# Down projections: one 512-column matmul into two banks' halves, or two 256-column matmuls into one sum

## The chip, the cores and the metric
The kernel runs on one core of one Trainium2 chip. The metric is the device time of one execution in microseconds (us); lower is better. It is one program: a decoder trunk of two layers, batch 1, 256 tokens, width 2048, all data in float32.

## The reference, cut to what matters
Nine products of the trunk end in an update of the residual stream x, each with a gate vector per feature:

```
x = x + g1 * ((u * sv) @ w_out)            # gMLP mixer, layer 0: 4096 -> 2048 features
x = x + g1 * (attention @ w_o)             # layer 1: 2048 -> 2048
x = x + g2 * ((silu(a) * v) @ w_down)      # both layers: 5632 -> 2048
```

The kernel calls all of them down projections (kind `dn`). The two gMLP halves (2048 rows each), the attention output, and for each layer three slices of the feed-forward (2048, 2048 and 1536 rows) make nine phases: `sgu_o0`, `sgu_o1`, `wo`, `dn00` to `dn02`, `dn10` to `dn12`. The rest of the trunk (up projections, key/value and query projections, spatial mixing, attention, the norms and the modulation vectors) isn't touched by the change.

## The kernel before, in words
**Precision.** Each float32 operand is split into a high half, which is what the type float32r holds, and a low half, the rest. A product is high weights times high activations, high weights times low activations, and low weights times high activations. Activations lie as `[128, tile, 512]`: columns 0 to 255 are the high half of the 256 tokens, 256 to 511 the low half (`h_op` for inputs of up projections, `act_op` for those of down projections).

**Weights.** All weights come as one stream of 1 MB pieces into four slots (`raw`). SyncE issues the loads and waits on the semaphore `stream`, which VectorE raises when it has done with half a piece. ScalarE rounds each half piece into `w_hi` (L923), VectorE subtracts it to get `w_lo` (L1091), four slots each. Between them come pieces of the modulation matrices, which VectorE multiplies and sums by itself (L1107). The order of weight halves (`s`), modulation pieces (`m`) and work on the previous chunk's result (`E`, `U`) is written out by hand for each chunk as a string of tokens, such as `sssEsEsEsmmssEm`; every engine walks the same strings.

**Tiling.** A chunk is 512 output features, four tiles of 128 (`TPC`). A down phase has four chunks, of eight half pieces each (six in `dn02` and `dn12`), 36 chunks and 272 half pieces in all. A half piece carries two tiles (k = 0, 1) of the inner dimension. For each of the four output tiles j, TensorE does two matmuls of 512 columns with the high weights (L1518) and then two of 256 columns with the low weights (L1522). Each has its own weight load. So in the bank of an output tile, columns 0 to 255 gather hi x hi and lo x hi, columns 256 to 511 gather hi x lo. That makes 2176 matmuls of each line on `act_op`. Chunks alternate between banks 0 to 3 and 4 to 7, so the result of one is read while the next is computed.

**Updating x.** VectorE's `update_x` (L1195) adds a chunk's result to x. For each output tile it does two instructions (L1211), one for each half of the bank: x = gate * half + x. It is 8 instructions a chunk, 288 in all. Normally, at the token `E` with number 0 of the next chunk it does the four for the first halves (`UPDATES[0]`), at number 1 the four for the second (`UPDATES[1]`), which raise `xlow`. The bank group is free again for TensorE when `xlow` has been raised four times for the chunk (`free_rule`, L236). At the token `U`, and where the next phase begins with a norm of x (`up00`, `kv`, `up10`), all eight are done together (`"all"`). After the last chunk both groups run, one behind the other, and the output transfers wait for `xlow`.

**Start of a phase with a norm.** ScalarE squares the last four tiles of x as `xlow` releases them (L965), TensorE sums the squares over partitions (L1433, L1436), ScalarE takes the root (L968), VectorE inverts it (L1155) after two weight halves, then both write the new `h_op` (L1175, L974, L1181). The first matmuls of the phase (L1506, L1509) wait for that.

Of the kernel before, what the change touches and what calls it, by code (L numbers as in the profile page):

```python
# [26 lines left out]
P = 128  # L27
D = 2048
T = 256
# [15 lines left out]
TPC = COLS // P  # L45
# [8 lines left out]
ALU, ACT, AX = mybir.AluOpType, mybir.ActivationFunctionType, mybir.AxisListType  # L54
# [229 lines left out]
def build(nc, io, stop=None):  # L284
# [7 lines left out]
    with ctx:  # L292
# [11 lines left out]
        x = sb("x_res", [P, KT, T])  # L304
# [20 lines left out]
        banks = ctx.enter_context(nc.psum_tensor("banks", [P, 8, 512], F32))  # L325
# [19 lines left out]
        def sem(name):  # L345
            return ctx.enter_context(nc.semaphore(name))
# [42 lines left out]
        prod = sem("prod")  # L389
        ahi = sem("ahi")  # L390
        alo = sem("alo")
        xup = sem("xup")
        xlow = sem("xlow")
        vread = sem("vread")
        v_copied = sem("v_copied")
# [51 lines left out]
        def vec(slice_, kt):  # L447

            return modv[:, slice_, kt:kt + 1] if isinstance(kt, int) else modv[:, slice_, bass.ds(kt, 1)]
# [51 lines left out]
        def done_wait(eng, prev):  # L501
# [2 lines left out]

        UPDATES = {0: [(0, j) for j in range(TPC)], 1: [(1, j) for j in range(TPC)],
                   "all": [(0, 0), (0, 1), (1, 0), (0, 2), (1, 1), (0, 3), (1, 2), (1, 3)]}

        def h_tiles(e):  # L510

# [563 lines left out]
        def _(dve):  # L1075
# [119 lines left out]
            def update_x(which, prev):  # L1195

                g = group(prev)
                gate, n = GATE_OF[PHASE_OF[id(prev.first)]], prev.first.n["xup"]
                if which != 1:
                    dve.wait_ge(mod_ready, ready_after(gate))  # L1200
                    if n:
                        dve.wait_ge(xlow, TPC * n)
                for part, j in UPDATES[which]:
                    if part:
                        dve.wait_ge(xup, TPC * n + j + 1)
                    elif j < TPC - 1:
                        dve.wait_ge(tile_done, (TPC - 1) * n + j + 1)
                    else:
                        done_wait(dve, prev)
                    kt = TPC * prev.first.loc + j  # L1210
                    dve.scalar_tensor_tensor(  # L1211
                        out=x[:, kt, :], in0=banks[:, g + j, T * part:T * (part + 1)], scalar=vec(gate, kt),
                        in1=x[:, kt, :], op0=ALU.mult, op1=ALU.add).then_inc(xlow if part else xup, 1)

            def evacuate(e, name, cur, prev, first):

# [171 lines left out]
        def _(pe):  # L1388
# [32 lines left out]
            def step(name, cur, prev, first):  # L1421
# [20 lines left out]
                for tok, t in enumerate(cur.first.tokens):  # L1442
# [8 lines left out]
                    if kind in ("v", "kvt", "vh"):  # L1451

                        pair, g = (u, g) if kind != "vh" else (2 * cur.first.loc + u % 2, 2 * (u // 2))
                        fresh_k, last_k = 0, KT - 1
                        if kind == "vh":
                            run = [r for r in range(5) if RUN_STARTS[r] <= cur.first.hs][-1]
                            fresh_k = 4 * BY_NAME["head"][RUN_STARTS[run]].loc
                            last_k = 4 * BY_NAME["head"][RUN_ENDS[run]].loc + 3
                            if u < 2:
                                pe.wait_ge(h_ready, 2 * (pair + 1))  # L1460
                            if run and cur.first.hs == RUN_STARTS[run] and u % 2 == 0:
                                if run <= 2:
                                    pe.wait_ge(v_copied, 4 * (run - 1) + u // 2 + 1)
                                else:
                                    pe.wait_ge(v_added, 4 * (run - 3) + u // 2 + 1)
                        hi = w_hi[:, slot, :].rearrange("p (k c) -> p k c", k=2)
                        lo = w_lo[:, slot, :].rearrange("p (k c) -> p k c", k=2)
                        for n in range(2):
                            for k in range(2):
                                kt = 2 * pair + k  # L1470
                                a_hi, a_lo = (operand[:, kt, o + P * n:o + P * (n + 1)] for o in (0, T))
                                out = banks[:, g + n, :]
                                pe.matmul(out, a_hi, hi[:, k, :], start=(kt == fresh_k), stop=False,  # L1473
                                          skip_group_check=True)
                                pe.matmul(out, a_hi, lo[:, k, :], start=False, stop=False, skip_group_check=True)  # L1475
                                last = pe.matmul(out, a_lo, hi[:, k, :], start=False, stop=(kt == last_k),  # L1476
                                                 skip_group_check=True)
                    elif kind == "gate":
                        hi = w_hi[:, slot, 0:KT * NGATE].rearrange("p (k c) -> p k c", k=KT)
                        lo = w_lo[:, slot, 0:KT * NGATE].rearrange("p (k c) -> p k c", k=KT)  # L1480
                        for kt in range(KT):
                            pe.matmul(banks[0:NGATE, g, :], hi[:, kt, :], operand[:, kt, :], start=(kt == 0),
                                      stop=False, skip_group_check=True)
                            last = pe.matmul(banks[0:NGATE, g, 0:T], lo[:, kt, :], operand[:, kt, 0:T],
                                             start=False, stop=(kt == KT - 1), skip_group_check=True)
                    elif kind == "cmp":
                        hi = w_hi[:, slot, :].rearrange("p (l c) -> p l c", l=8)
                        lo = w_lo[:, slot, :].rearrange("p (l c) -> p l c", l=8)
                        i = u // 4
                        for k in range(8):  # L1490
                            row = 8 * (u % 4) + k
                            rows = blk_view(i)[:, row, :]
                            pe.matmul(banks[:, g + i, 0:2 * NB], hi[:, k, :], rows, start=(row == 0), stop=False,
                                      skip_group_check=True)
                            last = pe.matmul(banks[:, g + i, 0:NB], lo[:, k, :], rows[:, 0:NB], start=False,
                                             stop=(row == CMP_LEN - 1), skip_group_check=True)
                    else:
                        hi = w_hi[:, slot, :].rearrange("p (k c) -> p k c", k=2)
                        lo = w_lo[:, slot, :].rearrange("p (k c) -> p k c", k=2)
                        last_kt = 2 * cur.first.nsub - 1  # L1500
                        if first and u == 0 and name in H_OF:
                            for k in range(2):
                                if k:
                                    pe.wait_ge(h_ready, KT * h_index(name) + 2)
                                for j in range(TPC):
                                    pe.matmul(banks[:, g + j, :], hi[:, k, P * j:P * (j + 1)], operand[:, k, :],  # L1506
                                              start=(k == 0), stop=False, skip_group_check=True)
                                for j in range(TPC):
                                    last = pe.matmul(banks[:, g + j, 0:T], lo[:, k, P * j:P * (j + 1)],  # L1509
                                                     operand[:, k, 0:T], start=False, stop=False,  # L1510
                                                     skip_group_check=True)
                            last.then_inc(sub_done, 1)
                            u += 1
                            continue
                        for j in range(TPC):
                            for k in range(2):
                                kt = 2 * u + k
                                pe.matmul(banks[:, g + j, :], hi[:, k, P * j:P * (j + 1)], operand[:, kt, :],  # L1518
                                          start=(kt == 0), stop=False, skip_group_check=True)
                            for k in range(2):  # L1520
                                kt = 2 * u + k
                                last = pe.matmul(banks[:, g + j, 0:T], lo[:, k, P * j:P * (j + 1)],  # L1522
                                                 operand[:, kt, 0:T], start=False, stop=(kt == last_kt),
                                                 skip_group_check=True)
                            if kind == "dn" and u == cur.first.nsub - 1 and j < TPC - 1:
                                last.then_inc(tile_done, 1)
# [139 lines left out]
```

## Time and profile before

| what | value |
|---|---|
| median of 3 runs | 2592.27 us (2591.88, 2592.27, 2598.79) |
| span of the profiled execution, its own time in the profile | 2590.9 us |
| TensorE matmuls busy | 2513.3 us, 97% |
| TensorE weight loads busy | 2167.4 us, 84% |
| VectorE busy | 2152.9 us, 83% |
| ScalarE busy | 1252.1 us, 48% |
| GpSimd busy | 376.4 us, 15% |
| DMA | 685.49 MB, mean 265 GB/s |

No separate time is listed for the profiled execution beside its span. Busy time of a group of overlapping matmuls is counted once, so busy time divided by the count is not the mean duration of one.

### The profile page before, as it was taken

Reading aid. Unit: us, or ns where it says so; the run is one execution under the profiler, and the core shown is the slowest. Engines: PE = TensorE matmul, PEld = TensorE weight load, DVE = VectorE, ACT = ScalarE, POOL = GpSimd, SP = SyncE. Lnnn points to the kernel's source line nnn. Section 1 sums busy time; section 2 is a strip of 40 time slices with the busy share of each in tenths; the row PEclk is TensorE's granted clock in tenths of the full one; section 3 lists DMA queues with packets and bytes.
Section 4 is the critical chain, followed back from the end, with each engine's and each line's share of the span. In section 5 each row is a group of like instructions: output and inputs, shape, how many; then the busy total and the mean of one; then the engine's idle time right before and its main releaser. Section 6 shows DMA issues by size and latency. Waiting matters only on the chain.

```text
span 2590.9 us, 38545 instructions
## 1 busy us (share of the span) xinstructions
PE 2513.3 (97%) x14006; PEld 2167.4 (84%) x14006; DVE 2152.9 (83%) x2593; ACT 1252.1 (48%) x1654; POOL 376.4 (15%) x205
## 2 busy tenths in 40 slices
PE   6999999998999999999999999899999999999999
PEld 4878888887888888888878788688788888888887
DVE  7899898999999899988998877678989756765666
ACT  4436444535554355435544454573555435543553
POOL 0000110231120012001142200373112001200110
PEclk8999999999999999999999979899999999999999
DMA  9998788986878877887766868207677655555554
GB/s 372 368 377 321 269 329 328 338 326 245 307 283 318 324 285 283 307 330 277 283 247 249 324 250 329 103 1 293 264 287 274 238 186 195 180 193 192 182 178 147
DMA packets 94312, 685.49 MB, mean 265 GB/s; under 512 B 10465, under 2 KB 10465, under 8 KB 11233
## 3 DMA queue, kind: packets, MB, share of 16 engines
q1 hardware_dynamic: 93746, 681.27, 70.1%
q10 hardware_dynamic: 432, 2.38, 0.2%
q8 instruction: 91, 1.49, 0.2%
q14 instruction: 43, 0.35, 0.0%
HBM read 681.51 MB, written 2.10 MB: 264 GB/s over the span
## 4 chain that ended last, share of the span: by engine, by line
PE 78%; DVE 10%; DMA 6%; issue 2%; ACT 2%; POOL 0%; SPq 0%; DVEq 0%; ACTq 0%
PE banks L1518 48%; PE banks L1522 24%; DMA raw<-in_stream 6%; DVE raw L1107 3%; DVE w_lo L1091 3%; ACT w_hi L923 1%; PE banks L779 1%; PE banks L743 1%; PE banks L765 1%; DVE scratch L853 1%; PE banks L782 1%; DVE temp L1175 0%; PE banks L1473 0%; PE banks L1475 0%; PE banks L1476 0%
## 5 line engine op out<-in xcount | busy, mean ns | idle before, releaser
L923 ACT ACTIVATE w_hi<-raw 128x1024 fp32r<-128x1024 f32 x841 | 875.8, 1056 | 990.6 <-PE banks L1522 594.9
L1091 DVE TENSOR_TENSOR w_lo<-raw,w_hi 128x1024 fp32r<-128x1024 f32 x841 | 1089.9, 1318 | 309.9 <-ACT w_hi L923 307.8
L1518 PE MATMUL banks<-h_op,w_hi 128*128 128x512 f32 x3816 | 1203.0, 397 | 6.2 <-DVE w_lo L1091 5.5
L1522 PEld LDWEIGHTS banks<-h_op,w_lo 128*128 128x128 f32 x3816 | 719.0, 188 | 170.0
L1522 PE MATMUL banks<-h_op,w_lo 128*128 128x256 f32 x3816 | 752.1, 278 | 0.0
L1518 PE MATMUL banks<-act_op,w_hi 128*128 128x512 f32 x2176 | 685.8, 397 | 0.6 <-DVE act_op L1252 0.3
L1518 PEld LDWEIGHTS banks<-h_op,w_hi 128*128 128x128 f32 x3816 | 582.4, 189 | 8.4 <-issue 5.8
L1107 DVE CUSTOM_DVE_ANT_0 raw<-raw,c_all 128x2048 f32<-128x2048 f32 x224 | 554.0, 2489 | 15.7 <-ACT c_all L897 9.5
L1522 PEld LDWEIGHTS banks<-act_op,w_lo 128*128 128x128 f32 x2176 | 409.8, 188 | 96.8
L1522 PE MATMUL banks<-act_op,w_lo 128*128 128x256 f32 x2176 | 428.7, 278 | 0.0
L1518 PEld LDWEIGHTS banks<-act_op,w_hi 128*128 128x128 f32 x2176 | 332.1, 189 | 1.8 <-issue 0.9
L1343 POOL TENSOR_TENSOR temp<-temp 128x1024 f32<-128x1024 f32 x16 | 94.2, 5886 | 1156.0 <-DVE temp L1239 1156.0
L1473 PE MATMUL banks<-w_hi,h_op 128*128 128x512 f32 x320 | 127.7, 399 | 25.7 <-DVE w_lo L1091 25.7
L1475 PE MATMUL banks<-w_lo,h_op 128*128 128x512 f32 x320 | 126.4, 395 | 0.0
L1476 PE MATMUL banks<-w_hi,h_op 128*128 128x512 f32 x320 | 126.1, 394 | 0.0
L1211 DVE SCALAR_TENSOR_TENSOR x_res<-banks,mod_sums,x_res 128x256 f32<-128x256 f32 x288 | 118.3, 473 | 9.0 <-PE banks L1522 8.9
L1002 ACT ACTIVATE temp<-zpad,small 128x256 f32<-128x256 f32 x176 | 91.6, 591 | 36.8 <-DVE zpad L1229 36.8
L684 POOL TENSOR_SCALAR attn_area<-attn_area 128x15 f32<-128x15 f32 (+2 forms) x96 | 65.9, 702 | 224.1 <-DVE attn_area L674 222.6
L1473 PEld LDWEIGHTS banks<-w_hi,h_op 128*128 128x128 f32 x320 | 61.1, 191 | 41.5 <-DVE w_lo L1091 25.4
L1229 DVE TENSOR_TENSOR zpad<-banks,zpad 128x1024 f32<-128x1024 f32 x44 | 53.8, 1222 | 43.0 <-ACT zpad L996 43.0
L1234 DVE SCALAR_TENSOR_TENSOR temp<-zpad,small,temp 128x256 f32<-128x256 f32 x176 | 80.8, 482 | 3.3 <-ACT temp L1002 2.0
L1352 POOL TENSOR_TENSOR act_op<-temp,act_op 128x1024 f32 (+1 forms) x24 | 67.2, 2801 | 86.4 <-ACT act_op L1013 86.4
(162 smaller groups left out, 1379.7 us busy)
## 6 DMA issues: line engine op xcount, KB each, us to landing
raw<-in_stream SPq DMA_DIRECT2D x645, 1024.0 KB, 5.4
x_res<-in_x SPq DMA_DIRECT2D x1, 2048.0 KB, 11.3
out_x<-x_res SPq DMA_DIRECT2D x4, 512.0 KB, 5.0
mix_area<-in_w_s ACTq DMA_DIRECT2D x1, 1024.0 KB, 9.2
mix_area<-in_b_s ACTq DMA_DIRECT2D x1, 1024.0 KB, 13.8
small<-in_small SPq DMA_DIRECT2D x1, 682.0 KB, 16.3
attn_area<-in_pos ACTq DMA_DIRECT2D x1, 273.0 KB, 5.3
c_all<-in_c SPq DMA_DIRECT2D x1, 8.0 KB
```

The lines of the kernel that those rows point to most:

```text
L923: act.activation(w_hi[:, out, 0:n], raw[:, slot, half:half + n], ACT.Copy).then_inc(hi_ready, 1)
L1002: act.activation(y4[:, j, :], zpad[:, j, 2:T + 2], ACT.Identity, bias=conv_col(prev, None, j), scale=conv_col(prev, 2, j)).then_inc(tap2, 1)
L1091: dve.tensor_tensor(w_lo[:, out, 0:n], raw[:, slot, half:half + n], w_hi[:, out, 0:n].bitcast(F32), ALU.subtract).then_inc(stream, 2 if ch ...
L1107: dve.tensor_tensor_reduce(raw[:, slot, :], raw[:, slot, :], c_all[:, :], 1.0, 0.0, ALU.mult, ALU.add, out).then_inc(stream, 2)
L1211: dve.scalar_tensor_tensor(out=x[:, kt, :], in0=banks[:, g + j, T * part:T * (part + 1)], scalar=vec(gate, kt), in1=x[:, kt, :], op0=ALU.m ...
L1234: dve.scalar_tensor_tensor(out=y4[:, j, :], in0=zpad[:, j, 1:1 + T], scalar=conv_col(prev, 1, j), in1=y4[:, j, :], op0=ALU.mult, op1=ALU.a ...
L1343: pool.tensor_tensor(y, y, gt, ALU.mult).then_inc(prod, 1)
L1473: pe.matmul(out, a_hi, hi[:, k, :], start=(kt == fresh_k), stop=False, skip_group_check=True)
L1475: pe.matmul(out, a_hi, lo[:, k, :], start=False, stop=False, skip_group_check=True)
L1476: last = pe.matmul(out, a_lo, hi[:, k, :], start=False, stop=(kt == last_k), skip_group_check=True)
L1518: pe.matmul(banks[:, g + j, :], hi[:, k, P * j:P * (j + 1)], operand[:, kt, :], start=(kt == 0), stop=False, skip_group_check=True)
L1522: last = pe.matmul(banks[:, g + j, 0:T], lo[:, k, P * j:P * (j + 1)], operand[:, kt, 0:T], start=False, stop=(kt == last_kt), skip_group_c ...
```

## The change
The high weights of a down projection meet the high and the low half of the activations in two matmuls of 256 columns, each with its own weight load, and both add into columns 0 to 255 of the bank. The second half of the bank is no longer used. `update_x` then does one instruction for each tile, four a chunk, all at token `E` number 0 (or at `U`, or at the end), and these raise `xlow`; the semaphore `xup` is gone.

```diff
-        UPDATES = {0: [(0, j) for j in range(TPC)], 1: [(1, j) for j in range(TPC)],
-                   "all": [(0, 0), (0, 1), (1, 0), (0, 2), (1, 1), (0, 3), (1, 2), (1, 3)]}
+        UPDATES = {0: range(TPC), 1: (), "all": range(TPC)}
...
-                for part, j in UPDATES[which]:
-                    if part:
-                        dve.wait_ge(xup, TPC * n + j + 1)
-                    elif j < TPC - 1:
+                for j in UPDATES[which]:
+                    if j < TPC - 1:
                         dve.wait_ge(tile_done, (TPC - 1) * n + j + 1)
                     else:
                         done_wait(dve, prev)
                     kt = TPC * prev.first.loc + j
                     dve.scalar_tensor_tensor(
-                        out=x[:, kt, :], in0=banks[:, g + j, T * part:T * (part + 1)], scalar=vec(gate, kt),
-                        in1=x[:, kt, :], op0=ALU.mult, op1=ALU.add).then_inc(xlow if part else xup, 1)
+                        out=x[:, kt, :], in0=banks[:, g + j, 0:T], scalar=vec(gate, kt),
+                        in1=x[:, kt, :], op0=ALU.mult, op1=ALU.add).then_inc(xlow, 1)
...
                                 kt = 2 * u + k
+                                if kind == "dn":
+                                    for part in range(2):
+                                        pe.matmul(banks[:, g + j, 0:T], hi[:, k, P * j:P * (j + 1)],
+                                                  operand[:, kt, T * part:T * (part + 1)],
+                                                  start=(kt == 0 and part == 0), stop=False, skip_group_check=True)
+                                    continue
                                 pe.matmul(banks[:, g + j, :], hi[:, k, P * j:P * (j + 1)], operand[:, kt, :],
                                           start=(kt == 0), stop=False, skip_group_check=True)
```

## Rows read from the trace of the kernel before

**Rows 1.** The page: busy time by engine; the TensorE clock granted in 40 slices.
```profile
PE 2513.3 (97%) x14006; PEld 2167.4 (84%) x14006; DVE 2152.9 (83%) x2593; ACT 1252.1 (48%) x1654; POOL 376.4 (15%) x205
PEclk8999999999999999999999979899999999999999
```
**Rows 2.** The page: the chain that ended last, by line.
```profile
PE banks L1518 48%; PE banks L1522 24%; DMA raw<-in_stream 6%; DVE raw L1107 3%; DVE w_lo L1091 3%; ACT w_hi L923 1%; PE banks L779 1%; PE banks L743 1%; PE banks L765 1%; DVE scratch L853 1%; PE banks L782 1%; DVE temp L1175 0%; PE banks L1473 0%; PE banks L1475 0%; PE banks L1476 0%
```
**Rows 3.** Groups of the span: count, busy us, mean ns, idle before.
```profile
L1518 PE MATMUL banks<-act_op,w_hi 128*128 128x512 f32 x2176 | 685.8, 397 | 0.6 <-DVE act_op L1252 0.3 <-DVE w_lo L1091 0.2
L1522 PE MATMUL banks<-act_op,w_lo 128*128 128x256 f32 x2176 | 428.7, 278 | 0.0
L1522 PEld LDWEIGHTS banks<-act_op,w_lo 128*128 128x128 f32 x2176 | 409.8, 188 | 96.8
L1506 PE MATMUL banks<-h_op,w_hi 128*128 128x512 f32 x24 | 11.7, 638 | 14.4 <-DVE h_op L1181 14.4
L1211 DVE SCALAR_TENSOR_TENSOR x_res<-banks,mod_sums,x_res 128x256 f32<-128x256 f32 x288 | 118.3, 473 | 9.0 <-PE banks L1522 8.9
```
**Rows 4.** Groups of TensorE within `dn10`, 2028 to 2116 us.
```profile
L1518 PE MATMUL banks<-act_op,w_hi 128*128 128x512 f32 x254 | 79.8, 395 | 0.0
L1522 PE MATMUL banks<-act_op,w_lo 128*128 128x256 f32 x252 | 49.6, 278 | 0.0
```
**Rows 5.** Timeline of matmuls and loads in `dn10`: start us, length us, x merged.
```profile
2050.16 0.63 PE L1518 MATMUL banks<-act_op,w_hi 128*128 128x512 f32 x2
2050.62 0.40 PE L1522 MATMUL banks<-act_op,w_lo 128*128 128x256 f32 x2
2050.86 0.63 PE L1518 MATMUL banks<-act_op,w_hi 128*128 128x512 f32 x2
...
2050.74 0.31 PEld L1518 LDWEIGHTS banks<-act_op,w_hi 128*128 128x128 f32 x2
```
**Rows 6.** Windows `sgu_o0`, `dn10`: length, PE, PEld, DVE, ACT, POOL busy, PEclk, DMA.
```profile
332.00:421.00 89.00, 89.00 (x513) 77.72 (x512) 78.89 (x84) 36.58 (x35) 5.01 (x2) 1.00 0.87 335
...
2028.00:2116.00 88.00, 88.00 (x507) 76.76 (x506) 54.08 (x67) 37.78 (x38) 0.00 (x0) 1.00 0.55 200
```
**Rows 7.** Groups of TensorE, 248 to 265 us: the spatial mixing.
```profile
L1539 PE MATMUL banks<-mix_area,scratch 128*128 128x128 f32 x128 | 14.7, 276 | 1.9 <-DVE scratch L853 1.9
```
**Rows 8.** Timeline from `sgu_o1` to `up00`.
```profile
598.74 3.21 DVE L1211 SCALAR_TENSOR_TENSOR x_res<-banks,mod_sums,x_res 128x256 f32<-128x256 f32 x8
...
599.86 0.40 PE L1522 MATMUL banks<-act_op,w_lo 128*128 128x256 f32 x2
...
601.60 0.81 ACT L965 ACTIVATE temp<-x_res 128x256 f32<-128x256 f32 x2 [0.37 <-DVE x_res L1211]
...
604.44 1.75 DVE L1155 RECIPROCAL rstd<-rstd 128x256 f32<-128x256 f32 x1
...
607.97 2.04 PE L1506 MATMUL banks<-h_op,w_hi 128*128 128x512 f32 x4 [4.77 <-DVE h_op L1181]
```
**Rows 9.** Timeline from `dn02` to `kv`, and from `wo` to `up10`.
```profile
1349.84 3.23 DVE L1211 SCALAR_TENSOR_TENSOR x_res<-banks,mod_sums,x_res 128x256 f32<-128x256 f32 x8 [1.73 <-PE banks L1522]
...
1351.03 0.39 PE L1522 MATMUL banks<-act_op,w_lo 128*128 128x256 f32 x2
...
1837.99 3.22 DVE L1211 SCALAR_TENSOR_TENSOR x_res<-banks,mod_sums,x_res 128x256 f32<-128x256 f32 x8
...
1839.17 0.40 PE L1522 MATMUL banks<-act_op,w_lo 128*128 128x256 f32 x2
```
**Rows 10.** Timeline of the end of the kernel.
```profile
2585.38 0.39 PE L1522 MATMUL banks<-act_op,w_lo 128*128 128x256 f32 x2
...
2585.80 2.05 DVE L1211 SCALAR_TENSOR_TENSOR x_res<-banks,mod_sums,x_res 128x256 f32<-128x256 f32 x5 [0.21 <-PE banks L1522]
...
2587.88 0.33 SPq L889 DMA_DIRECT2D out_x<-x_res  x1
```

More of the change, by code:

```diff
@@ L391, in build @@
         alo = sem("alo")
-        xup = sem("xup")
         xlow = sem("xlow")
```

## The prediction
> **What bounds the kernel now.** I read the engine shares first: TensorE's matmuls are busy for 97% of the span, VectorE for 83% [rows 1]. The chain of waits agrees: 72% of it are the two matmul lines 1518 and 1522, and most of the rest is the weight stream of the first stages [rows 2]. Then the windows of single down phases, since that is where the change sits. In the densest of them for VectorE, `sgu_o0`, TensorE is busy for 89.00 of 89.00 us at a granted clock of 1.00, and VectorE for 78.89; in `dn10` it is 88.00 of 88.00 against 54.08 [rows 6]. The 2176 high matmuls on `act_op` have 0.6 us of idle time before them in the whole kernel [rows 3]. So in a down phase time is set by how often TensorE can start a matmul, and VectorE's updates lie beside it. Only at three changes of phase and at the end does TensorE stand still behind the updates [rows 8 to 10].
>
> **The matmuls.** What counts is the distance from one start to the next, not the recorded duration (397 and 278 ns), since they overlap. Two ways lead to it. Two merged matmuls are busy for one distance plus one duration. In `dn10`, line 1522 has 49.6 us for 252: 196.8 ns each, 393.7 a pair, less 278 is 115.7 ns. Line 1518 has 79.8 us for 254: 314.2 each, 628.3 a pair, less 395 is 233.3 ns [rows 4]. The timeline gives the same: two high ones take from 2050.16 to 2050.62, two low ones to 2050.86, so 0.70 us for a tile's four [rows 5]. The groups of all 2176 give 233.3 and 116.0 by the same working [rows 3].
>
> The change puts 2176 x 2 = 4352 matmuls of 256 columns where 2176 of 512 were, 2176 more with as many more weight loads. At 115.7 ns a piece the two take 231.4 ns where one took 233.3 to 233.5: 2.1 ns less, 2176 times, is 4.6 us less. It hangs on a small difference of two measured distances, so I bound it. Upper end: the starts are given in steps of 10 ns, so the pair of low ones from 2050.62 to 2050.86 may be 0.236 us or more [rows 5], 118 ns each; 2 x 118 less 233 is +3 ns, +6.5 us. Lower end: the 128-column matmuls of the spatial mixing take 14.7 us for 128, 114.8 ns each with the gap in them [rows 7]; if 113 is what a full 128-column load allows, it is -7.3 ns, -16 us.
>
> The new weight loads: does a load keep up with 116 ns, six times in a row, where it did so twice and then had 233 ns twice? A load is recorded with 188 ns [rows 3], more than 116, but the two loads recorded from 2050.74 together take 0.31 us, so the second began 0.12 us after the first, and they overlap [rows 5]. The spatial mixing had 128 loads and 128 matmuls of 128 columns in a row at 114.8 ns [rows 7]. So the pace is known to hold, also for the supply of instructions, which goes from 8 to 12 in 0.70 us, 58 ns each; the mixing used one every 57 ns. I cost the loads at nothing beyond the distance.
>
> TensorE's page of the Trainium skill speaks against the split. "TensorE: Matmul & The Clock Gate", section "Back-to-back issue gap", gives the gap at the full clock as columns over 2.4 GHz and 2.5 ns on top, for each matmul. By it, an estimate, two halves would cost 2.5 ns more than one whole, +5.4 us over 2176, and the sum below would come out 10 us higher. The trace has 115.7 and 233.3 instead, above the rule's 109 and 216, and shows no fixed part: twice the short distance is less than the long one [rows 4].
>
> **The updates.** 288 instructions take 118.3 us of VectorE, 0.41 us each in a row [rows 3]; half of them go, 59 us. In the middle of a phase that is worth nothing, because TensorE has no idle time there [rows 6]; its cover is TensorE's own row, and cover grows rather than shrinks. Nothing waits longer either: `xlow` comes four instructions earlier, so banks and GpSimd's squares are released sooner, and no wait is added. The stream gets its slots sooner; it only fills slots that TensorE doesn't need yet.
>
> At the three changes of phase the updates stand on the path: squares, sum, root, inverse and the new `h_op` all hang on the last `xlow` [rows 8]. From `sgu_o1` to `up00` eight updates run from 598.74 to 601.95. The last tile's sum is complete at about 600.26, the end of the pair at 599.86; the other three updates are done by about 599.97. The new last one starts at about 600.35 and ends at 600.82, 1.13 us earlier. From `dn02` to `kv`: sum complete at 1351.42, last update over at about 1352.0, against 1353.07: 1.05 us. From `wo` to `up10`: complete at 1839.57, over at 1840.1, against 1841.21: 1.1 us [rows 9]. All that comes after is a chain that moves as a whole, with the weight halves ahead of the inverse (604.44) moving too. Together 3.3 us. What is late next is the same chain with its root and inverse; TensorE's stop of 4.8 us before line 1506 [rows 8] stays as long, it only begins earlier. If the weight stream, not VectorE, were what holds `up00` afterwards, about 1 us of it would be lost again.
>
> At the end, five updates run from 2585.80 to 2587.85 and the last transfer is issued at 2587.88 [rows 10]. One is left, from 2585.80 to 2586.27: 1.6 us less.
>
> **Sum.** -4.6 - 3.3 - 1.6 = -9.5 us. Against the span of 2590.9 that is 2581.4. The median of the runs shown lies 1.4 above that span, so I forecast 2582.8, 0.37% less. A difference of 0.3%, 7.8 us, is about what a measurement of this kernel can tell from no change. The forecast lies close to it.
>
> **Rivals.**
> A, the halves cost what the whole did, or each a little more: distance 116.7 to 119. Then the matmuls give 0 to +10 us, and 4.9 us is still saved: 2587 to 2597, in the middle 2590, no difference. For it: the group of all low matmuls gives 116.0, not 115.7 [rows 3], and 233.5 is twice 116.7. The skill's fixed part per matmul (same page and section) would land here too, at an estimated 2592.8. Against it: every pair read is at or under 116. 32%.
> B, slower: the pace of the loads. The pairs of fast loads are followed by slow ones now, and a row of six may run out of what was loaded ahead. Its place is every high matmul of a down phase, its price the part of a load that shows: with the busy time per 256-column matmul (196.8) in place of the distance, 2 x 196.8 - 314.2 = 79 ns more, 2176 times, +172 us less the 4.9 us that is saved, 2759 at the far end. It cancels the 4.9 us from a distance of 117.8 ns on, and passes 0.3% from 119.6 ns; a middle case of 122 is +23 us less 4.9, 2610. For it: 188 ns recorded per load against 116. Against: rows 5 and 7. 9%.
> C, a larger gain: the halves run at the 113 to 114 ns that the short matmuls of rows 7 come close to, or TensorE comes back earlier to its full clock after the three stops. The 24 matmuls of line 1506 take 638 ns against 397 [rows 3], 5.8 us in all. At -12 us for the halves it is 2575. 14%.
> The forecast itself, 2579 to 2586: 45%.
>
> **How the numbers follow.** Time 2582.8. The range runs from C's middle to A's upper end, 2574 to 2597, and leaves out B and the far end of C. For faster by over 0.3% (under 2584.5) I count all of C, three quarters of the forecast and a little of A, which bends towards the lower distances: 0.52. Within 0.3%: 0.37. Slower by over 0.3%: 0.11, B and the last of A.
>
> **What would show it.** In the profile after: 4352 matmuls of 256 columns in place of 2176, with a busy time per piece in a down phase that is one distance, 115 to 116 ns, in a row of six. A window of 88 us in `dn10` then holds some 761 matmuls, not 507. Line 1211 has 144 instructions; the runs of eight at 598, 1349 and 1838 are four, and the last `xlow` comes about 0.5 us after the last matmul; the same holds for the end. VectorE's busy time is 59 us less, with no shorter down phase to show for it. The prediction is wrong if the distance in a down phase is over 117.8 ns (no gain), if loads appear with idle matmul time between them (B), or if a stop of TensorE before line 1506 becomes longer than 4.8 us, which would eat the 3.3 us.

## The result, and the profile after

The changed kernel takes 2613.1 us (median of 4 runs, 2610.45 to 2618.37), the kernel before 2593.51 us beside it. The ratio is 1.0073, 95% interval 1.0056 to 1.009. A second comparison (`a0_changed_again`, below) gave 1.0079, 1.0064 to 1.0094. So the change costs 0.7% to 0.8%, some 20 us, where 9.5 us less was forecast. The time lies above the range (2574 to 2597).

The page of the changed kernel: busy time by engine, and the granted clock.
```profile
span 2608.7 us, 42753 instructions
...
PE 2532.5 (97%) x16182; PEld 2286.8 (88%) x16182; DVE 2086.6 (80%) x2449; ACT 1253.9 (48%) x1654; POOL 356.4 (14%) x205
...
PEclk8999999999999999999999979899999999999999
```
Against [rows 1]: 2176 more loads and matmuls, 66 us less of VectorE, the same clock row. The span is 17.8 us longer and TensorE is busy 19.2 us longer. So the lost time is in TensorE's work, and the groups say in which.

The groups of the span, as in [rows 3].
```profile
L1516 PE MATMUL banks<-act_op,w_hi 128*128 128x256 f32 x4352 | 699.8, 283 | 0.0
L1524 PE MATMUL banks<-act_op,w_lo 128*128 128x256 f32 x2176 | 438.4, 283 | 0.0
L1207 DVE SCALAR_TENSOR_TENSOR x_res<-banks,mod_sums,x_res 128x256 f32<-128x256 f32 x144 | 60.7, 477 | 16.9 <-PE banks L1524 16.3
L1502 PE MATMUL banks<-h_op,w_hi 128*128 128x512 f32 x24 | 10.1, 561 | 13.2 <-DVE h_op L1179 13.2
```
The two groups of matmuls on `act_op` were busy for 685.8 + 428.7 = 1114.5 us before; now they are busy for 699.8 + 438.4 = 1138.2 us, 23.7 us more. There is no idle time before them.

The window of `dn10` that answers to [rows 6]. Columns are length, PE, PEld, DVE, ACT, POOL busy (count), PEclk, DMA share and GB/s.
```profile
2040.00:2128.00 88.00, 88.00 (x736) 88.00 (x735) 48.69 (x54) 36.40 (x37) 0.00 (x0) 1.00 0.56 196
```
Its timeline, as in [rows 5]: start, length, instruction, x merged.
```profile
2050.24 0.64 PE L1516 MATMUL banks<-act_op,w_hi 128*128 128x256 f32 x4
2050.72 0.40 PE L1524 MATMUL banks<-act_op,w_lo 128*128 128x256 f32 x2
2050.96 0.64 PE L1516 MATMUL banks<-act_op,w_hi 128*128 128x256 f32 x4
```
A window counts every matmul that lies in it even in part, so the distance between starts is window plus one duration over the count: 88.28 us / 736 = 119.9 ns. (One matmul more or less in the count moves a distance by 0.2 ns here and by 0.5 ns in the windows of 512 columns below, and a tile of a window of 88 us by 1 to 1.4 ns.) The timeline agrees: four from 2050.24, two from 2050.72, the next at 2050.96, six in 0.72 us. A tile takes 720 ns. Before it was (88.00 + 0.3) / 507 x 4 = 696.6 ns [rows 6]. 761 matmuls in 88 us had been forecast. The loads are now busy for all of the window.

The change from `sgu_o1` to `up00`, as in [rows 8].
```profile
605.14 0.40 PE L1524 MATMUL banks<-act_op,w_lo 128*128 128x256 f32 x2
...
612.08 1.58 PE L1502 MATMUL banks<-h_op,w_hi 128*128 128x512 f32 x4 [4.38 <-DVE h_op L1179]
```
From the start of the last pair of down matmuls to the first of the next phase it is 6.94 us, against 607.97 - 599.86 = 8.11 us: 1.17 us less, where 1.13 was forecast. Of this, 0.39 us is a shorter stop before the first matmul, 4.38 us against 4.77; the forecast had the stop as long as before. The same distance at the other two changes shrank by 1.11 us each, counted from the start of the last down matmul (6.90 and 6.82 us against 8.01 and 7.93), where 1.05 and 1.1 were forecast.

The end of the kernel, as in [rows 10].
```profile
2604.77 0.40 PE L1524 MATMUL banks<-act_op,w_lo 128*128 128x256 f32 x2
...
2605.72 0.33 SPq L887 DMA_DIRECT2D out_x<-x_res  x1
```
From the last pair to the last transfer it is 0.95 us against 2.50: 1.55 us less, 1.6 forecast.

### The profile page after: what moved, and what is told of

It reads as the page before. It is cut to its first block, busy times and chain, and to the rows that moved or that the text cites. A ratio compares the mean times of both kernels' runs of the same rounds, so it can differ in the third digit from the quotient of the medians.

```text
span 2608.7 us, 42753 instructions
## 1 busy us (share of the span) xinstructions
PE 2532.5 (97%) x16182; PEld 2286.8 (88%) x16182; DVE 2086.6 (80%) x2449; ACT 1253.9 (48%) x1654; POOL 356.4 (14%) x205
## 4 chain that ended last, share of the span: by engine, by line
PE 83%; DVE 8%; DMA 5%; issue 2%; ACT 2%; POOL 0%; SPq 0%; DVEq 0%; ACTq 0%
PE banks L1520 32%; PE banks L1524 26%; PE banks L1516 20%; DMA raw<-in_stream 5%; DVE raw L1105 2%; DVE w_lo L1089 2%; DVE temp L1173 1%; ACT w_hi L921 1%; PE banks L777 1%; PE banks L741 1%; PE banks L1469 1%; PE banks L1471 1%; PE banks L1472 1%; PE banks L763 1%; DVE scratch L851 1%
## 5 line engine op out<-in xcount | busy, mean ns | idle before, releaser
L1516 PE MATMUL banks<-act_op,w_hi 128*128 128x256 f32 x4352 | 699.8, 283 | 0.0
L1516 PEld LDWEIGHTS banks<-act_op,w_hi 128*128 128x128 f32 x4352 | 600.4, 192 | 0.5 <-issue 0.4
L1105 DVE CUSTOM_DVE_ANT_0 raw<-raw,c_all 128x2048 f32<-128x2048 f32 x224 | 545.7, 2452 | 14.2 <-ACT c_all L895 9.6
L1524 PE MATMUL banks<-act_op,w_lo 128*128 128x256 f32 x2176 | 438.4, 283 | 0.0
L1524 PEld LDWEIGHTS banks<-act_op,w_lo 128*128 128x128 f32 x2176 | 339.4, 192 | 0.0
L682 POOL TENSOR_SCALAR attn_area<-attn_area 128x15 f32<-128x15 f32 (+2 forms) x96 | 65.9, 703 | 228.3 <-DVE attn_area L672 226.7
L994 ACT ACTIVATE zpad<-banks 128x1024 f32<-128x1024 f32 x44 | 45.1, 1026 | 68.5 <-PE banks L1524 68.5
```

Source lines behind the costliest of these rows:

```text
L1105: dve.tensor_tensor_reduce(raw[:, slot, :], raw[:, slot, :], c_all[:, :], 1.0, 0.0, ALU.mult, ALU.add, out).then_inc(stream, 2)
L1516: pe.matmul(banks[:, g + j, 0:T], hi[:, k, P * j:P * (j + 1)], operand[:, kt, T * part:T * (part + 1)], start=(kt == 0 and part == 0), sto ...
```

## The experiments

### The two halves of the change, each alone

**Split, but two sums** (`e1_split_two_halves`), on the kernel before:
```diff
+                                if kind == "dn":
+                                    for part in range(2):
+                                        pe.matmul(banks[:, g + j, T * part:T * (part + 1)],
+                                                  hi[:, k, P * j:P * (j + 1)],
+                                                  operand[:, kt, T * part:T * (part + 1)],
...
```


> The kernel before with the high matmul cut into two of 256 columns, each still adding into its own half of the bank, and x updated in eight instructions as before. It is the split without the single sum. The profile of the changed kernel shows 120.0 ns from start to start in all six matmuls of a tile (720 ns) where the kernel before has 696.6. Theory F, a fixed part of about 13.3 ns for every load and matmul beyond its columns at 2.4 GHz (256 columns 106.7, 120.0 measured; 512 columns 213.3, 226.5 measured in the key and value projections before): 720 ns a tile, 1088 tiles, +25 us over before, some 2619 us, 5 us above the changed kernel. Theory L, a load of 128 columns can only follow the last one after 120 ns: the same 2619. Theory S, that adding into the same 256 columns one matmul after the other is slow: 697 ns a tile and 2593 us, as before.

Measured: 2618.78 us (5 runs), ratio to before 1.0088 (1.0073 to 1.0103). The same window of `dn10`:
```profile
2051.00:2139.00 88.00, 88.00 (x736) 88.00 (x735) 53.82 (x66) 35.80 (x37) 0.00 (x0) 1.00 0.53 191
```
736 again, 120 ns. Theory S is out: adding into one sum costs nothing that can be seen, and the split costs all. Over the whole kernel the split alone costs 22.8 us (18.9 to 26.7), where 1088 tiles at 23.4 ns would be 25.5.

**The updates alone** (`e2_one_update_alone`): the changed kernel without the `if kind == "dn":` block, so the high matmul has 512 columns again.

> The matmuls of before (one of 512 columns with the high weights), with the updates of the changed kernel: four a chunk, from the first half of the bank alone. It leaves out of x what the high weights make of the activations' low halves. It prices the other part of the change: -3.3 us at the three changes of phase and -1.6 us at the end, by the prediction, so 4.9 us less than before, about 2588.6 us, with 696.6 ns a tile. Rival: the later chain or the weight stream gives it back, less than 1.5 us from before.

Measured: 2589.75 us (12 runs), 0.9978 (0.9968 to 0.9988), 5.7 us less by the ratio. The 4.9 us of the prediction lie within the interval (3.1 to 8.3 us), and the rival (less than 1.5 us) is out. In its trace the three changes of phase and the end have the same lengths as in the changed kernel, to 0.01 us, and its window of `dn10` holds 507 matmuls in 88 us, as before. VectorE is busy 67 us less (2085.5 against 2152.9 us), and within the down phases that shortens nothing.

**The changed kernel again** (`a0_changed_again`), unchanged.

> The changed kernel as it is, beside the kernel before on this chip, to have its ratio from more runs: 1088 tiles at +23.4 ns is +25.5 us, the updates give back 5.4 us (e2), so about 20 us over before, a ratio of 1.0077.

Measured: 2614.13 us (6 runs), 1.0079 (1.0064 to 1.0094), 20.5 us. The halves account for it within the noise: 25.5 - 5.7 = 19.8 us with the split by count, 22.8 - 5.7 = 17.1 us with the split as e1's times have it, against 16.6 to 24.4 here.

### Half the dose, and the mixed row

**One of two split** (`e8_one_of_two_split`): as e1, with `if kind == "dn" and k == 1`.

> The kernel before with only one of the two high matmuls of a tile cut in two (inner tile k = 1), own halves, eight updates. It is half the dose: one load and matmul more a tile. A part of 13.3 ns for each load and matmul: 696.6 + 13 = 708 to 710 ns a tile, +12.5 to +14.5 us, some 2608 us. If the price comes only when six short ones stand in a row and a long one lets the loads catch up, the tile stays at 697 and the time at 2595.

Measured: 2606.93 us (one run, beside 2595.28 before).
```profile
2039.00:2127.00 88.00, 88.00 (x621) 82.63 (x620) 53.50 (x67) 36.27 (x37) 0.00 (x0) 1.00 0.54 191
```
88.3 / 621 x 5 = 711 ns a tile: 14 ns for the first additional load and matmul, and 9 more for the second (720). So it isn't only six short ones in a row that cost: one more pair of load and matmul is paid for even with a long matmul left in each tile.

**All four at 512 columns** (`e3_all_512_columns`), on the kernel before:
```diff
-                                last = pe.matmul(banks[:, g + j, 0:T], lo[:, k, P * j:P * (j + 1)],
-                                                 operand[:, kt, 0:T], start=False, stop=(kt == last_kt),
+                                cols = HILO if kind == "dn" else T
+                                last = pe.matmul(banks[:, g + j, 0:cols], lo[:, k, P * j:P * (j + 1)],
+                                                 operand[:, kt, 0:cols], start=False, stop=(kt == last_kt),
```


> The kernel before with the low weights' matmuls of a down phase widened from 256 to 512 columns (they add low x low into the second half, which the reference's product holds too), so all four matmuls of a tile have 512. Reading 1, that 233 and 116 ns in the row of before are true prices of 512 and 256 columns: 4 x 233.3 = 933 ns a tile, +257 us, 2852 us. Reading 2, that each load and matmul pays 13.3 ns beyond its columns and the starts in the mixed row are recorded unevenly (2 x 226.7 + 2 x 120 = 693, measured 696.6): 226.7 each, 907 ns a tile, +229 us, 2824 us.

Measured: 2819.8 us (one run).
```profile
2183.00:2296.00 113.00, 113.00 (x501) 93.58 (x500) 54.64 (x67) 36.60 (x37) 0.00 (x0) 1.00 0.42 152
```
113.39 / 501 = 226.3 ns each, 905 ns a tile; Reading 1 (933) is out. This is the run that explains the miss. In the row of before a matmul of 512 columns seemed to take 233 ns; in a row of its own kind it takes 226.3, and one of 256 columns takes 120, not 116. The distances within a mixed row aren't the prices of its members. A uniform row stood in the trace of before, in the first phase (with activations as the loaded operand and weights as the moving one), and I hadn't used it. Its timeline, three lines in turn:
```profile
140.08 0.39 PE L1473 MATMUL banks<-w_hi,h_op 128*128 128x512 f32 x1
...
146.88 0.39 PE L1473 MATMUL banks<-w_hi,h_op 128*128 128x512 f32 x1
```
30 matmuls of 512 columns in 6.80 us are 226.7 ns each. Against the 120.0 of a uniform row of 256, that is 106.7 ns for 256 columns more: one column for each cycle of 2.4 GHz, the clock that a granted 1.00 stands for. So 213.3 of the 226.7 ns are columns and 13.3 stay, and of the 120.0 ns 106.7 are columns and 13.3 stay. That part comes once for each load and matmul, and the split adds one.

### What the part beyond the columns hangs on

**280 columns** (`e5_280_columns`), on the changed kernel: `o = (T - 24) * part`, `banks[:, g + j, 0:280]`, `operand[:, kt, o:o + 280]`, and 280 for the low weights too.

> The changed kernel with 280 moving columns in place of 256 in every matmul of a down phase (the second of the two takes columns 232 to 511): sums of the wrong columns, so the result is not the product. 280 columns at 2.4 GHz are 116.7 ns. Theory F: 116.7 + 13.3 = 130 ns from start to start, 780 ns a tile, +65 us over the changed kernel, 2678 us. Theory L: still under the pace of the loads, 120 to 121 ns, 2613 to 2619 us.

Measured: 2668.21 us (one run).
```profile
2080.00:2176.00 96.00, 96.00 (x748) 96.00 (x747) 49.10 (x55) 36.38 (x37) 0.00 (x0) 1.00 0.49 177
```
96.29 / 748 = 128.7 ns: 24 columns (10 ns) more cost 8.8 ns more. Theory L, a pace of 120 set by the loads, is out. Theory F has the sign and most of the size (12.0 instead of 13.3 beyond the columns).

**Narrower weights.** `e4_weights_64_columns` has `hi[:, k, P * j:P * j + 64]` into `banks[0:64, ...]`, low weights likewise; `e7_weights_32_columns` the same with 32; `e10_weights_64_all_512` is e3 with 64.

> The changed kernel with weight blocks of 64 columns in place of 128 in every matmul of a down phase: output features 64 to 127 of each tile are left out. It halves what a load has to bring and leaves the moving columns at 256. Theory F (fixed part for a load and matmul, whatever it loads): still about 120 ns from start to start, some 2613 us. Theory L (the loads set the pace of 120): the loads take half, so the moving columns decide, 107 to 111 ns, 640 to 666 ns a tile, 55 to 85 us less, 2530 to 2560 us.

> As e4, with weight blocks of 32 columns: output features 32 to 127 of each tile of a down phase are left out. So far the part beyond the moving columns (106.7 ns for 256) was 13.3 ns with 128 weight columns and 6.7 ns with 64. Theory P, the part is in proportion to the weight columns: 3.3 ns, 110.0 from start to start, 660 ns a tile, 1088 tiles, some 2559 us. Theory C, a constant 6.7 ns and from 64 columns on something else on top: 113.3 as with 64 columns, 2579 us.

> The kernel with all four matmuls of a tile at 512 moving columns (e3: 906.7 ns a tile), now with weight blocks of 64 columns: output features 64 to 127 of each tile of a down phase are left out. Theory P (a part of each load is paid whatever the matmul beside it): 213.3 + 6.7 = 220.0 ns, 880 ns a tile, 29 us less than with 128 weight columns, 2791 us. Theory L in its last form (a load only shows where the matmul beside it is short, and under 512 columns it is covered; the 13.3 there is another cost): 226.7 ns, 907 a tile, 2820 us.

Measured, one run each: 2579.16, 2590.4 and 2830.59 us. Their windows of `dn10`, in this order:
```profile
2019.00:2104.00 85.00, 85.00 (x752) 85.00 (x751) 48.77 (x54) 37.34 (x38) 0.00 (x0) 1.00 0.57 203
```
```profile
2025.00:2113.00 88.00, 88.00 (x750) 80.72 (x748) 49.15 (x55) 36.95 (x38) 0.00 (x0) 1.00 0.54 193
```
```profile
2189.00:2303.00 114.00, 114.00 (x497) 66.54 (x496) 54.04 (x66) 36.66 (x37) 0.00 (x0) 1.00 0.41 150
```
That is 85.28 / 752 = 113.4 ns with 64 weight columns, 88.28 / 750 = 117.7 with 32, and 114.39 / 497 = 230.2 with 64 beside 512 moving columns. None of the expectations holds. Half the load took 6.6 ns off a short matmul, a quarter of it took only 2.3 off, and at 512 columns half the load made it 3 to 4 ns slower than e3. (Fewer weight columns also mean fewer partitions of the bank written, so these runs don't change the load alone.) So the part is neither constant nor in proportion to the load; it stays between 7 and 17 ns in every row tried. e4 matches no theory: F said 120, L said 107 to 111. It does exclude one more rival: with the same number of instructions it ran at 113.4 ns, so the supply of instructions isn't what sets 120.

### The order of the row

**Long and short in turn** (`e12_long_short_in_turn`): the two `for k` loops of a tile merged into one, everywhere.

> The kernel before with another order of the four matmuls of a tile, in the down phases and everywhere else that uses these two lines: 512, 256, 512, 256 columns in place of 512, 512, 256, 256. The same matmuls, loads and columns. So far the part beyond the columns was 13.3 ns in uniform rows (256: 120.0; 512: 226.7), 14.2 in the row of before, and with narrower weights it went up as well as down (113 to 118 for 256 columns, 230 for 512). If it belongs to each matmul alone, the order changes nothing: 696.6 ns a tile, within 0.1% of before. If it hangs on which matmul stands beside which load, the tile moves: each ns is 3.0 us over the 2996 tiles of the kernel, so 693 ns would be -11 us, 700 ns +10 us.

Measured: 2616.15 us (6 runs), 1.0071 (1.0055 to 1.0087).
```profile
2045.00:2133.00 88.00, 88.00 (x500) 76.28 (x499) 53.80 (x66) 37.03 (x38) 0.00 (x0) 1.00 0.54 191
```
88.3 / 500 x 4 = 706 ns a tile: +10 ns for the same four matmuls. So the part beyond the columns isn't a fixed price that each matmul brings along; it hangs on the neighbours too.

**Rows of four and of eight** (`e13_rows_of_four`, `e14_rows_of_eight`), on the kernel before; the first loop holds the high matmuls, the second the low ones, and `e14` has 4 in place of 2:
```diff
+                        per = 1 if kind == "dn" and u == cur.first.nsub - 1 else 2
+                        for j0 in range(0, TPC, per):
+                            for j in range(j0, j0 + per):
...
+                            for j in range(j0, j0 + per):
...
```


> The kernel before, same matmuls, in rows of four long (two tiles' high ones) and four short (their low ones), everywhere the two lines are used but in the last half piece of a down chunk, which keeps its order. Changes between long and short: one per tile in place of two (before) or four (e12). Theory W (each load and matmul has 13.3 ns beyond its columns, and each change of width costs on top: before 696.6 less 693.3 is 3.3 ns for two changes, e12 706.6 less 693.3 is 13.3 for four): 695 ns a tile, some 4 to 5 us under before. Theory B (what costs is a change of bank, or the same bank twice): this order has the same banks in the same pairs, but returns to each bank, so twice the changes of bank: slower than before.

> As e13 with all four tiles together: eight long, eight short. Theory W: half a change a tile, 694.1 ns, 7 us under before. Theory B: as e13, slower than before. If the uniform 13.3 is reached only in rows without any change, about before.

Measured: 2604.49 us, 1.0035 (1.0024 to 1.0046), and 2597.52 us, 1.0007 (0.9997 to 1.0017), 12 runs each. One up phase (`up11`) in e13, in e14 and in the kernel before:
```profile
2128.00:2304.00 176.00, 176.00 (x1006) 153.83 (x1006) 117.46 (x131) 92.14 (x106) 20.76 (x6) 1.00 0.51 186
```
```profile
2123.00:2299.00 176.00, 176.00 (x1009) 154.87 (x1009) 117.78 (x131) 92.90 (x106) 20.93 (x6) 1.00 0.52 186
```
```profile
2118.00:2294.00 176.00, 176.00 (x1013) 153.57 (x1012) 118.08 (x133) 93.23 (x106) 21.06 (x6) 1.00 0.52 186
```
By count, 701, 699 and 696 ns a tile. Theory W wanted e13 4 to 5 us and e14 7 us below before. e13 is above, and e14 can't be told from before by its time, but 7 us less (0.9973) is outside its interval; Theory W falls. Theory B has the sign for e13, but not for e14 (which changes banks as often and is nearly level) nor for e12 (same banks in the same order, yet the slowest). Neither explains the row.

The trace of e14 shows one thing more, in a timeline of an up phase:
```profile
2200.10 2.00 PE L1520 MATMUL banks<-h_op,w_hi 128*128 128x512 f32 x8
2201.94 1.11 PE L1526 MATMUL banks<-h_op,w_lo 128*128 128x256 f32 x8
2202.90 1.32 PE L1520 MATMUL banks<-h_op,w_hi 128*128 128x512 f32 x5
```
Eight short ones take 0.96 us, 120 ns each, though long ones stand on both sides; eight long ones take 1.84 us, 230 ns each. The 116 ns of the row of before belongs to a pair of short ones between long ones and isn't kept in a longer row of them.

### Versions meant to be faster

**Updates in another order** (`e6_updates_reordered`): in `"all"`, `(1, 2)` goes ahead of `(0, 3)`, and the end of the kernel uses `"all"`.

> The matmuls of before and all eight updates, but with two instead of three left behind the last matmul of a phase before a norm (the second half of tile 2 comes before the first half of tile 3), and at the end of the kernel two instead of five. By the update rows of before (0.41 us each in a row): 3 x 0.4 + 3 x 0.41 = 2.4 us less than before, some 0.1%. The updates of the changed kernel alone gave 0.22% (e2). Rival: the extra wait of the last update on the one just ahead of it eats the 0.4, and only the 1.2 us of the end are left.

Measured: 2593.75 us (11 runs), 0.9996 (0.9987 to 1.0005). No difference can be told; by the times alone the 2.4 us (0.9991) aren't excluded. The trace says where they went. From the last pair (at 2589.43) to the last transfer (at 2591.46) it is 2.03 us against 2.50 [rows 10], 0.5 us less where 1.2 was expected: two updates of 0.41 us for each tile of 0.70 us pile up behind the last tiles in this order. At the first change of phase it is 8.24 us (603.99 to 612.23) against 8.11, 0.13 us longer where 0.4 less was expected, and 0.12 to 0.13 longer at the other two. Together nothing is left.

**The change in four chunks** (`e9_split_in_last_chunks`), on the kernel before:
```diff
+        def summed_once(at):
+            return at.first.kind == "dn" and at.first.loc == 3 and \
+                PHASE_OF[id(at.first)] in ("sgu_o1", "dn02", "wo", "dn12")
...
+                                if summed_once(cur):
+                                    for part in range(2):
+                                        pe.matmul(banks[:, g + j, 0:T], hi[:, k, P * j:P * (j + 1)],
...
```


> The change in the last chunk of four phases alone (sgu_o1, dn02, wo and dn12), where the updates stand on the path; all other chunks as before. 8 + 6 + 8 + 6 = 28 half pieces, 112 tiles at 23.4 ns more each (720 less 696.6) is +2.6 us; the updates give the 5.4 us back that the kernel with one update alone (e2) showed. Together 2.8 us less than before, about 0.1%. If the price of the split were not in the matmuls of a chunk but in something the whole phase pays, it would be slower than before.

Measured: 2591.13 us (11 runs), 0.9984 (0.9975 to 0.9993). The forecast, 0.9989, lies in the interval. This version beats both kernels: the split is paid on 112 tiles, and the updates' gain is whole, since the three changes of phase and the end are as short in its trace as in the changed kernel's, to 0.01 us.

**Both** (`e15_rows_of_eight_and_e9`).

> e14 together with the change in four last chunks alone (e9, which gave 0.16% over before). Theory W: 7 + 4 = 11 us under before, 0.4%, 2584 us. Theory B: the gain of e9 is lost and more.

Measured: 2595.5 us (12 runs), 1.0006 (0.9995 to 1.0017). Theory W's 0.996 is out, and no gain is left. That the rows of eight take back what e9 gives fits this, but e14 (1.0007) and e15 can't be told apart.

## Why the prediction was wrong

**The step that failed is the term of the matmuls.** It was -4.6 us, with bounds of -16 and +6.5. By the periods it measured 1088 x 23.4 = +25.5 us, by the times of e1 +22.8 (18.9 to 26.7). The prediction took the distances of 115.7 and 233.3 ns in a mixed row as prices, and put the 256-column one into a row of its own. e3 shows that a 512-column matmul costs 226.3 in a row of its own, and the changed kernel that a 256-column one costs 120. The upper bound rested on the same distances, read with 10 ns steps, so it wasn't a bound from elsewhere. What was there to be read is the period of the whole row: 696.6 ns for 1536 columns (640 ns) is 14.2 ns for each of four. One more load and matmul per 512 columns at that price is +28 ns a tile; by the uniform row of the first phase it is 6 x 120.0 - 696.6 = +23.4. The sum also counted the high matmuls alone. The two low ones of a tile went from 115.7 to 120 ns as well, 8.6 of the 23.4 ns, and the prediction had no term for them.

**The sentence of the Trainium skill was right in sign.** The traces have 13.3 ns beyond the columns in uniform rows of 256 and of 512. The prediction set a fixed part aside because twice 115.7 is less than 233.3. The page of the Trainium skill that it named, "TensorE: Matmul & The Clock Gate", section "Back-to-back issue gap", has a part of each matmul beyond its columns too, 2.5 ns; by it the sum was 2592.8. That section calls its formula the gap of a single matmul by itself, and says that in a stream of loads and matmuls both set the spacing; the prediction left this out. The rows here are such a stream. They confirm a part beyond the columns, at five times the formula's figure; that it is the same part isn't shown.

**Loads at nothing beyond the distance.** The mixing's 114.8 ns [rows 7] (112 from start to start; busy time over count is a little more) showed that loads and instructions can come that fast, but its moving operands are 128 columns of plain float32. It said nothing of 256 columns of float32r. The loads didn't open idle time between the matmuls (0.0 in both groups), as rival B had it, yet the distance passed B's two points, 117.8 for no gain and 119.6 for slower. Both points counted the high matmuls alone. With all six at one distance against 696.6, the gain is gone from 116.9 ns on and 0.3% is lost from 118.0. B's sign held; its mechanism isn't shown, since e5 excludes a fixed pace of the loads and e4, e7 and e10 fit no simple rule.

**The updates: right.** 3.3 + 1.6 = 4.9 us were forecast, 5.7 (3.1 to 8.3) measured in e2. 1.17, 1.11 and 1.11 us at the changes of phase and 1.55 at the end, 4.9 together, stand in the profile against 1.13, 1.05, 1.1 and 1.6. VectorE's 66 us less in the page shortened no down phase (e2). It was 59 by the update rows; line 1211 went from 118.3 to 60.7 us, 57.6, the rest is other lines.

**The rivals.** A (2587 to 2597) pointed the right way, stopped at 119 ns a matmul, 1 ns short, and left the low matmuls out too. Of C, that TensorE comes back earlier to its full clock is not shown: the 24 matmuls behind the three stops had a mean of 561 ns in the page above and 638 before, but 616 in the second profile of the same changed kernel (a0) and 622 in e2. The chances (0.11 for slower) leaned on the three readings of one mixed row that agreed with each other because they were one measurement.

**What stays open** is what the part beyond the columns is made of. It depends on the order and on the widths of the row (13.3 uniform, 14.2 before, 16.6 long and short in turn), and on the width of the weights without a direction. A matmul without its load wasn't tried, so load and matmul can't be told apart; the two halves of the split use the same weights, so that run would also say whether a split could be made cheap.

## What to carry to other kernels

Price a TensorE instruction by the period of a whole repeating row, and only for a row of the same make; the distance between two neighbours in a mixed row can be 7 ns off (233.3 against 226.3), 15 us over the 2176 matmuls here, more than the whole forecast. A split of a matmul that keeps its columns costs a load and matmul more (9 to 14 ns here), so do it only where what it saves is on the path, as in the four chunks of e9. In this kernel, where TensorE has no idle time within a down phase, saved VectorE work is worth what it shortens behind the last matmul of a phase, and nothing elsewhere.

## What the runs showed of the hardware

- Each float32r load and matmul, with 128 weight columns at the granted clock of 1.00, took 13.3 ns (256 columns) and 13.0 to 13.4 ns (512) beyond its columns at 2.4 GHz in uniform rows.
- The order of the same four matmuls moves the tile from 696.6 to 706 ns. None of the three other orders tried is faster than that of before; rows of eight (699 ns) can't be told from it by time.
- Matmuls of 256 columns follow each other at 116 ns in pairs between pairs of 512 (before), and at 120 ns in a row of eight between rows of 512 (e14) or in a row of their own.
- Weights of 64 columns made 256-column matmuls 6.6 ns faster (e4) and 512-column ones 3 to 4 ns slower (e10, one run each).
- 6528 accumulations into one half of a bank, six in a row on the same columns, cost nothing against two halves (e1: the same 120 ns from start to start).
